# A fourth of the tokens take their value rows by index: the last matrix phase of a DiT block with 16,384 single-neuron experts

## The chip, the cores and the metric

The kernel runs on one core of one Trainium2 chip, as one program. The metric is the time of one execution on the device in microseconds (us); of several runs the median counts. The engines of the core are named as in the profile: PE is TensorE (matrix products; PEld its weight loads), DVE is VectorE, ACT is ScalarE, POOL is GpSimd, and SP issues most transfers.

## The reference

One transformer block is computed for 256 latent tokens of width 2048 (with 256 context tokens beside them in the attention part). What matters here is its last part, an expert layer in which each expert is one pair of rows, u and v. For each token, 8 heads choose 16 of 16,384 experts each, so 128 experts per token:

```
def peer(h, w_q, sub_keys, u, v):
    ...
    top_s, pos = lax.top_k(cand, PEER_TOPK)
    idx = jnp.take_along_axis(cidx, pos, axis=-1)
    g = jax.nn.softmax(top_s, axis=-1)
    ...
        act = jax.nn.gelu(jnp.einsum('cd,ced->ce', hc, u_sel))
        wts = (gc * act.astype(jnp.float32)).astype(v.dtype)
        return jnp.einsum('ce,ced->cd', wts, v[ic])
```

The expert index is a pair (i1, i2), each from 0 to 127: i1 names a tile of 128 experts, i2 the row in it. After this part come the gated residual (the gate g2 is one of six vectors that a product with w_ada gives, the "ada" vectors) and a final RMS norm.

## The kernel before, in words

The kernel does not look rows up. It computes all 16,384 experts for all 256 tokens, and zeroes what was not chosen. The weights of all phases lie one after another in one array, `stream`, in units of 128x1024 f32 (512 KB), and SP loads them in that order into a ring of four buffers (`raw`). Each unit is two halves of 128x512. For each half, ACT writes the rounded high part (`w_hi`, L367), DVE the rest (`w_lo`, L1008), and PE multiplies; there are four slots for split halves, so ACT and DVE work at most four halves ahead of PE. A product is made of three matmuls in fp32r (L668): high x high, high x low and low x high. The counters `w_high`, `w_low` and `w_free` order this by halves.

**U phase** (`first_product`, 128 tiles). Each tile of 128 experts takes four halves of 12 matmuls of 128x256 (256 tokens are the moving columns). ACT applies GELU. Before tile 2 x ROUTE_AT the result goes into `A` ([128 experts, 128 tiles, 256 tokens]); from then on `route` also runs: for each group of four tokens, four f32 matmuls of one-hot tables (L925) give a 128x128 table of gates, and DVE multiplies it into `A` (L1450). With 64 groups, one for each of the 64 tiles from tile 64 on, the gates of all 256 tokens are in `A` when the phase ends.

**V phase** (from `open_banks(experts_in)` on, 128 tiles). Each tile again takes four halves. Now the experts' values are the stationary operand and the weights the 512 moving columns: for each half and each of two blocks of 128 tokens, three matmuls of 128x512 into the eight PSUM banks, which stay open over all tiles. The values of each tile are split into `p_hi` (ACT, L614) and `p_lo` (DVE, L1481). DVE's loop body is `value_turn`: two tiles, so eight halves of `w_lo` and two of `p_lo`. In 32 of these turns it also adds one piece of w_ada into a sum (`acc_v`, L1505); the pieces come in through SP's queue between the units.

**Tail.** The banks are copied to `y_tok`, 16 small f32 products with a vector of ones turn the ada sum into columns (`ada_columns`, L675), 32 transposes (L986) bring the result back to the feature-major layout, DVE adds the residual (L1540), and the norm and four stores follow. POOL does little: it zeroes sums, and makes the distances for the one-hot tables (L349).

## Time and profile before

| what | value |
|---|---|
| median of 3 runs | 2293.31 us (2292.7 to 2295.07) |
| the profiled execution's own time | 2292.91 us |
| its span, first to last instruction | 2291.1 us |
| PE busy | 2211.5 us, 97% of the span |
| DVE busy | 1587.5 us, 69% |
| ACT busy | 1211.5 us, 53% |
| POOL busy | 100.2 us, 4% |
| mean granted TensorE clock | 0.987 |
| moved by DMA | 453.26 MB, mean 198 GB/s |

Busy time is the sum of an engine's instruction durations with overlaps counted once, so that an engine whose instructions overlap can be busy all the time and still have room. For what one instruction costs in a row of its like, read the distance between starts. The chain of work that ended last tells which engine sets the time of each stretch; the windows tell how much room the others have.

### The profile page before, as it was taken

How to read it: one execution, taken by the hardware profiler on the slowest of the kernel's cores; microseconds unless marked ns; L12 is line 12 of the kernel's file. 1: busy time of each engine (PE TensorE's matmuls, PEld its weight loads, DVE VectorE, ACT ScalarE, POOL GpSimd, SP SyncE). 2: the span in 40 equal slices, each digit the busy share in tenths (PEclk: the TensorE clock that was granted, in tenths of full speed). 3: DMA queues.
4: the chain of work that ended last, by engine and by line, in shares of the span. 5: the costliest groups of instructions: out<-in, count | busy, mean ns of one | idle time of the engine just before them, and what ended most of it. 6: DMA issues, size and time to landing. Idle time of an engine off the chain costs nothing.

```text
span 2291.1 us, 43555 instructions
## 1 busy us (share of the span) xinstructions
PE 2211.5 (97%) x14034; PEld 1952.9 (85%) x14034; DVE 1587.5 (69%) x2903; ACT 1211.5 (53%) x2131; POOL 100.2 (4%) x87
## 2 busy tenths in 40 slices
PE   4899999899999999999999999999999999999997
PEld 0478887668989999999999999998888888888886
DVE  5377767786674688788578788785666666555554
ACT  3232234575454677777665565655555555555553
POOL 0000000000000000000211111110000000000000
PEclk8899999899999999999999999999999999999998
DMA  9878876202755455555544444445766766555652
GB/s 387 338 268 282 281 251 235 99 1 76 275 200 183 150 176 187 183 182 183 169 157 162 156 156 162 157 157 210 248 238 238 242 243 238 193 193 193 193 193 81
DMA packets 123891, 453.26 MB, mean 198 GB/s; under 512 B 14400, under 2 KB 15168, under 8 KB 123200
## 3 DMA queue, kind: packets, MB, share of 16 engines
q1 hardware_dynamic: 123840, 452.63, 58.1%
q8 instruction: 26, 0.43, 0.1%
q14 instruction: 25, 0.20, 0.0%
HBM read 448.38 MB, written 4.19 MB: 198 GB/s over the span
## 4 chain that ended last, share of the span: by engine, by line
PE 92%; DVE 4%; DMA 2%; issue 1%; ACT 0%; SPq 0%; DVEq 0%
PE PS L668 84%; PE PS L925 3%; DMA ada_t<-w_ada 1%; PE PS L824 1%; DVE st L1209 1%; PE PS L798 1%; PE PS L675 1%; PE PS L711 1%; PE PS L651 1%; DMA raw<-stream 1%; PE PS L812 1%; PE PS L912 0%; DVE ot L1544 0%; DVE oT_l L1322 0%; DVE O L1254 0%
## 5 line engine op out<-in xcount | busy, mean ns | idle before, releaser
L367 ACT ACTIVATE w_hi<-raw 128x512 fp32r<-128x512 f32 x1296 | 816.7, 631 | 901.8 <-PE PS L668 891.0
L1008 DVE TENSOR_TENSOR w_lo<-raw,w_hi 128x512 fp32r<-128x512 f32 x1296 | 884.5, 691 | 557.8 <-ACT w_hi L367 542.1
L668 PE MATMUL PS<-h_h,w_hi 128*128 128x256 f32 (+1 forms) x2304 | 657.8, 285 | 2.1 <-DVE h_l L1038 2.1
L668 PE MATMUL PS<-h_h,w_lo 128*128 128x256 f32 (+1 forms) x2304 | 651.8, 283 | 0.0
L668 PE MATMUL PS<-h_l,w_hi 128*128 128x256 f32 (+1 forms) x2304 | 651.7, 283 | 0.0
L668 PEld LDWEIGHTS PS<-h_h,w_hi 128*128 128x128 f32 x2304 | 441.9, 192 | 3.1 <-issue 2.6
L668 PEld LDWEIGHTS PS<-h_l,w_hi 128*128 128x128 f32 x2304 | 442.1, 192 | 0.0
L668 PEld LDWEIGHTS PS<-h_h,w_lo 128*128 128x128 f32 x2304 | 441.8, 192 | 0.0
L668 PE MATMUL PS<-w_hi,p_hi 128*128 128x512 f32 x1024 | 398.5, 389 | 0.0
L668 PE MATMUL PS<-w_hi,p_lo 128*128 128x512 f32 x1024 | 398.3, 389 | 0.0
L668 PE MATMUL PS<-w_lo,p_hi 128*128 128x512 f32 x1024 | 398.3, 389 | 0.0
L668 PEld LDWEIGHTS PS<-w_hi,p_hi 128*128 128x128 f32 x1024 | 192.2, 188 | 40.3 <-DVE p_lo L1481 0.4
L668 PEld LDWEIGHTS PS<-w_lo,p_hi 128*128 128x128 f32 x1024 | 192.2, 188 | 39.9
L668 PEld LDWEIGHTS PS<-w_hi,p_lo 128*128 128x128 f32 x1024 | 192.2, 188 | 39.9
L668 PE MATMUL PS<-w_hi,hl_h 128*128 128x512 f32 x288 | 113.9, 396 | 3.3 <-DVE w_lo L1008 3.3
L668 PE MATMUL PS<-w_lo,hl_h 128*128 128x512 f32 x288 | 113.3, 393 | 0.0
L668 PE MATMUL PS<-w_hi,hl_l 128*128 128x512 f32 x288 | 113.0, 392 | 0.0
L1023 DVE SCALAR_TENSOR_TENSOR acc<-ada,silu_c,acc 128x1024 f32<-128x1024 f32 x80 | 102.5, 1281 | 3.4
L349 POOL TENSOR_TENSOR hotB<-iota,i2T 128x512 f32<-128x512 f32 x64 | 78.0, 1219 | 371.4 <-PE PS L925 339.2
L1450 DVE TENSOR_TENSOR A<-A,PS 128x512 f32 (+1 forms) x64 | 87.9, 1374 | 0.0
L668 PE MATMUL PS<-w_hi,hc_h 128*128 128x512 f32 x160 | 65.5, 409 | 12.4 <-DVE w_lo L1008 12.4
L668 PE MATMUL PS<-oT_h,w_hi 128*128 x256 | 72.5, 283 | 0.0
(198 smaller groups left out, 2250.6 us busy)
## 6 DMA issues: line engine op xcount, KB each, us to landing
raw<-stream SPq DMA_DIRECT2D x648, 512.0 KB, 3.4
ada<-w_ada SPq DMA_DIRECT2D x96, 512.0 KB, 4.5
ada_t<-w_ada SPq DMA_DIRECT2D x64, 512.0 KB, 9.4
ada_v<-w_ada SPq DMA_DIRECT2D x32, 512.0 KB, 4.3
x_c<-x_ctx SPq DMA_DIRECT2D x1, 2048.0 KB, 7.7
x<-x_lat SPq DMA_DIRECT2D x1, 2048.0 KB, 15.1
x_scratch<-x SPq DMA_DIRECT2D x1, 2048.0 KB, 7.3
x<-x_scratch SPq DMA_DIRECT2D x1, 2048.0 KB, 8.6
```

The costliest lines, as they stand in the source:

```text
L349: nc.gpsimd.tensor_tensor(hotB[:], iota[:].unsqueeze(1).broadcast_to([P, 4, P]), i2T[:, bass.ds(t0, 4)].unsqueeze(2).broadcast_to([P, 4, P ...
L367: nc.scalar.activation(w_hi[:, (2 * j + hf) % SPLIT, :], raw[:, j, hf * HALF:(hf + 1) * HALF], ACT.Copy).then_inc(S["w_high"], 1)
L651: ins = mm(PS[:, NORM_BANK[r], 0:T], ones_sq[:], s[:, k, :], start=(k == 0), stop=(k == KT - 1))
L668: ins = mm(out_, l_, r_, start=(start and q == 0), stop=(stop and q == 2), skip_group_check=check)
L675: ins = mm(PS[:, bank, at_ + k:at_ + k + 1], total[:, c % 2, k * P:(k + 1) * P], ones[:], start=True, stop=True)
L711: ins = mm(PS[32 * j:32 * j + 2, ADA1_BANK[g % 2], :], silu_c[:, kt + j // 2, :], ada1_t[(n + j // 2) % ADA1][:, j % 2 * HALF:(j % 2 + 1) ...
L798: ins = mm(PS[:, 2 * qt + sub, :], q, kT[sub * DH:(sub + 1) * DH, k, :], start=True, stop=True)
L812: ins = nc.tensor.transpose(PS[:, 4 + s % 2, k * P:(k + 1) * P], pr[:, m % 2, slot, k * P:(k + 1) * P], ident[:])
L925: ins = mm(PS[:, 4 + s, q * P:(q + 1) * P], hotB[:, q, :], hotA[:, q, :], start=True, stop=True)
L1008: V_.tensor_tensor(w_lo[:, h % SPLIT, :], raw[:, h // 2 % RAW, at_:at_ + HALF], w_hi[:, h % SPLIT, :].bitcast(F32), ALU.subtract).then_inc ...
L1023: ins = V_.scalar_tensor_tensor(acc[:, c % 2, :], ada[:, kt % ADA, :], silu_c[:, kt, 0:1], acc[:, c % 2, :], ALU.mult, ALU.add)
L1450: V_.tensor_tensor(av, av, PS[:, 4 + s, :].rearrange("p (t i) -> p t i", t=4), ALU.mult).then_inc(S["routed"], 1)
```

## The change

The 256 tokens are parted: DENSE = 192 and PICKED = 64.

- V phase, tokens 0 to 127: as before, three matmuls of 128x512 for each half.
- V phase, tokens 128 to 191: their low and high parts stand side by side in one stationary tile of 128 columns (`p_hl`), so that two matmuls, with `w_hi` and with `w_lo`, do for them. The two parts of each token end in different PSUM partitions and are added in the tail, by a product with `fold` (two identities of 64, one over the other).
- V phase, tokens 192 to 255: no matmul. POOL fetches their chosen rows of v by index, from `stream` in DRAM. One step j fetches one chosen row for each of 64 tokens x 2 halves of their list, so 128 rows of 8 KB, in two indirect DMAs of 128x1024, and DVE adds weight x row into `mixed` (two instructions of 128x1024, L1592). There are 64 steps and four row buffers. The weights need the GELU values of these tokens: ACT stores that part of `A` to DRAM (`values`; two stores, of 128x80x64 and 128x48x64 f32, the second at the end of the U phase), and POOL fetches it back with 64 indirect DMAs of 128 single numbers (`picked`), in four groups of 16.
- Routing covers 48 groups of four tokens instead of 64, and begins at tile 80 instead of 64 (ROUTE_AT 40 instead of 32).
- The last 32 pieces of w_ada, added by DVE during the V phase before, are now added in the U phase, over eight of PE's double tiles from LATE_ADA_AT = 30 on, and the 16 small `ada_columns` products stand there too, not in the tail.
- About eleven small DVE instructions in the U phase make the indices. The residual comes back at another place of SP's queue.

The core of the diff:

```diff
@@ sync @@
+            for r in range(8):
+                units(34 + LATE_ADA_AT + r)
+                for q in range(ADA):
+                    ...
+                    sp.dma_start(ada_u[:, q, :], w_ada_flat[64 + n]).then_inc(ada_in[q], 16)
...
@@ gpsimd @@
+            def fetch_rows(j):
+                for hf, index in enumerate((row_near.bitcast(U32), row_far)):
+                    nc.gpsimd.indirect_dma_start(
+                        row_t[:, j % ROWS, hf * UNIT:(hf + 1) * UNIT], None, rows,
+                        bass.IndirectOffsetOnAxis(ap=index[:, j:j + 1], axis=0)).then_inc(row_in[j % ROWS], 16)
+            def fetch_value(j):
+                nc.gpsimd.indirect_dma_start(
+                    picked[:, j:j + 1], None, singles,
+                    bass.IndirectOffsetOnAxis(ap=value_at.bitcast(U32)[:, j:j + 1], axis=0)
+                    ).then_inc(pick_in[j // PICK_GROUP], 16)
+            pool.wait_ge(S["picks_in"], 48)
+            pool.wait_ge(S["far_ready"], 1)
+            pool.wait_ge(S["w_free"], 2 * U_V + SPLIT)
+            for j in range(ROWS):
+                fetch_rows(j)
+            pool.wait_ge(S["values_kept"], 32)
+            for j in range(PICK_GROUP):
+                fetch_value(j)
+            for j in range(ROWS, PICKED):
+                pool.wait_ge(S["mixed"], 2 * (j - ROWS) + 4)
+                fetch_rows(j)
+                for k in range(PICK_GROUP + 2 * (j - ROWS), min(PICK_GROUP + 2 * (j - ROWS) + 2, PICKED)):
+                    fetch_value(k)
@@ scalar @@
+            nc.scalar.dma_start(values[:, 0:2 * ROUTE_AT, :], A[:, 0:2 * ROUTE_AT, DENSE:T]).then_inc(S["values_kept"], 16)
...
+            act.wait_ge(S["gelu_in"], NE_TILES - 2 * ROUTE_AT + 2)
+            nc.scalar.dma_start(values[:, 2 * ROUTE_AT:NE_TILES, :], A[:, 2 * ROUTE_AT:NE_TILES, DENSE:T]
+                                ).then_inc(S["values_kept"], 16)
@@ tensor @@
-                    for t in range(QT):
-                        tok = slice(t * P, (t + 1) * P)
-                        ins = three(PS[:, 4 * t + h % 4, :], p_hi[:, i, tok], p_lo[:, i, tok], slice(0, HALF),
-                                    h % SPLIT, False, False, check=True)
+                    three(PS[:, h % 4, :], p_hl[:, i, 0:P], p_hl[:, i, DENSE:DENSE + P], slice(0, HALF), h % SPLIT,
+                          False, False, check=True)
+                    both = p_hl[:, i, DENSE + P:2 * DENSE + PICKED]
+                    for w in (w_hi, w_lo):
+                        ins = mm(PS[:, 4 + h % 4, :], both, w[:, h % SPLIT, :], start=False, stop=False,
+                                 skip_group_check=True)
...
-            ada_columns(6, 3, acc_v)
-            ada_columns(7, 3, acc_v, 8)
...
+                if c == 0:
+                    pe.wait_ge(S["mixed"], 2 * PICKED + 2)
...
-                    for t in range(QT):
-                        ins = nc.tensor.transpose(turned(k)[:, t * P:(t + 1) * P], y_tok[:, t, k * P:(k + 1) * P], ident[:])
+                    nc.tensor.transpose(turned(k)[:, 0:P], y_tok[:, 0, cols], ident[:])
+                    mm(turned(k)[:, P:DENSE], y_tok[:, 1, cols], fold[:], start=True, stop=True)
+                    ins = mm(turned(k)[:, DENSE:T], mixed[:, cols], fold[:], start=True, stop=True)
@@ vector @@
+            def mix(r, s, hf):
+                cols = slice(hf * UNIT, (hf + 1) * UNIT)
+                if hf == 0:
+                    dve.wait_ge(row_in[s], 32 * r + 32)
+                dve.wait_ge(S["mixed"], 8 * r + (2 * s + hf + 1))
+                V_.scalar_tensor_tensor(mixed[:, cols], row_t[:, s, cols], weight[:, bass.ds(4 * r + s, 1)],
+                                        mixed[:, cols], ALU.mult, ALU.add).then_inc(S["mixed"], 1)
...
+            for b in range(3):
+                value_turn(0, b)
+            dve.wait_ge(S["values_kept"], 32)
+            dve.wait_ge(S["p_high_too"], 8)
+            dve.wait_ge(S["p_low"], 8)
+            V_.memset(mixed[:], 0.0).then_inc(S["mixed"], 2)
+            for g in range(PICK_GROUPS):
+                js = slice(g * PICK_GROUP, (g + 1) * PICK_GROUP)
+                dve.wait_ge(pick_in[g], 16 * PICK_GROUP)
+                link(V_.tensor_tensor(weight[:, js], picked[:, js], gate_at[:, js], ALU.mult))
+                bodies = PICK_GROUP // 4 - (g == PICK_GROUPS - 1)
+                with dve.Fori(0, bodies) as r:
+                    for s in range(4):
+                        value_turn(4 * r, 3 + g * PICK_GROUP + s, r + g * (PICK_GROUP // 4), s)
             split_low(161, 2)
             split_low(161, 3)
+            for s in range(4):
+                for hf in range(2):
+                    mix(PICKED // 4 - 1, s, hf)
```

PE, the first two halves of the V phase. Before, each half is two rounds of three matmuls, one for each block of 128 tokens:

```order
L668 MATMUL PS<-w_hi,p_hi 128x512
L668 MATMUL PS<-w_lo,p_hi 128x512
L668 MATMUL PS<-w_hi,p_lo 128x512
L668 MATMUL PS<-w_hi,p_hi 128x512
L668 MATMUL PS<-w_lo,p_hi 128x512
L668 MATMUL PS<-w_hi,p_lo 128x512
L966 REGISTER_ALU
```

PE, the same place after the change (L720 is the old L668; `p_hl` holds both parts of all 192 tokens):

```order
L720 MATMUL PS<-w_hi,p_hl 128x512
L720 MATMUL PS<-w_lo,p_hl 128x512
L720 MATMUL PS<-w_hi,p_hl 128x512
L1033 MATMUL PS<-w_hi,p_hl 128x512
L1033 MATMUL PS<-w_lo,p_hl 128x512
L1023 REGISTER_ALU
```

Five matmuls of the same shape stand where six stood, in each of 512 halves.

DVE, the start of the V phase after the change, with the counters that each instruction waits for (L1070 is the old L1008, L1583 the old L1481; three turns of 4 + 1 + 4 + 1 instructions stand ahead of the memset):

```order
L1070 TENSOR_TENSOR w_lo<-raw,w_hi 128x512 [waits w_high] x4
L1583 TENSOR_TENSOR p_hl<-A,p_hl 128x192 [waits p_high]
L1621 MEMSET mixed 128x2048 [waits p_high_too,p_low,values_kept]
L1625 TENSOR_TENSOR weight<-picked,gT 128x16 [waits pick_in0]
L1627 UNCONDITIONAL_BRANCH [waits dve]
L1627 ISA
L1070 TENSOR_TENSOR w_lo<-raw,w_hi 128x512 [waits w_high]
...
L1591 ISA [waits row_in0]
L1592 ISA [waits mixed]
L1592 SCALAR_TENSOR_TENSOR mixed<-row_t,weight,mixed 128x1024
```

After three turns DVE now waits for the stored values (`values_kept`) and for the first 16 fetched columns of them (`pick_in0`), with all later `w_lo` queued behind; then each turn has two instructions on `mixed`, the first of which waits for its row.

POOL, from the last one-hot distance on, after the change (before, one memset of `acc_v` stood here):

```order
L368 TENSOR_TENSOR hotB<-iota,i2T 128x512
L373 REGISTER_ALU
L373 COMPARE_AND_BRANCH
L383 DMA row_t<-stream,i1T 128x1024
L383 DMA row_t<-stream,row_far 128x1024
...
L388 DMA picked<-values_scratch,i2T 128x1 x16
L383 DMA row_t<-stream,i1T 128x1024
L383 DMA row_t<-stream,row_far 128x1024
L388 DMA picked<-values_scratch,i2T 128x1 x2
```

POOL issues 8 row fetches, then 16 value fetches, then 56 times two row fetches; the first 24 of these have two value fetches behind them.

## Rows read from the trace of the kernel before

**Rows 1.** The page, part 4: the chain that ended last, by engine and line.
```profile
PE 92%; DVE 4%; DMA 2%; issue 1%; ACT 0%; SPq 0%; DVEq 0%
PE PS L668 84%; PE PS L925 3%; DMA ada_t<-w_ada 1%; PE PS L824 1%; DVE st L1209 1%; PE PS L798 1%; PE PS L675 1%; PE PS L711 1%; PE PS L651 1%; DMA raw<-stream 1%; PE PS L812 1%; PE PS L912 0%; DVE ot L1544 0%; DVE oT_l L1322 0%; DVE O L1254 0%
```
**Rows 2.** The same chain in order of time: start us, us, what.
```profile
1208.97 0.89 PE PS L925 x8
1209.86 5.75 PE PS L668 x48
...
1559.35 1.90 PE PS L860 x8
1561.25 696.56 PE PS L668 x3072
2257.81 1.76 PE PS L864 x8
2260.24 5.17 PE PS L675 x32
```
**Rows 3.** Windows: stretch, us, busy (instructions) by engine, granted clock, DMA share, GB/s.
```profile
1000.00:1100.00 100.00, 100.00 (x834) 99.79 (x833) 77.96 (x144) 71.14 (x105) 13.23 (x8) 1.00 0.58 185
...
1700.00:1800.00 100.00, 100.00 (x442) 82.79 (x442) 66.77 (x102) 52.18 (x92) 0.00 (x0) 1.00 0.70 242
...
2100.00:2200.00 100.00, 100.00 (x443) 82.81 (x442) 57.09 (x93) 52.61 (x93) 0.00 (x0) 1.00 0.60 194
```
**Rows 4.** DVE's timeline in the V phase: start us, us, instruction, idle before.
```profile
1699.14 1.28 DVE L1505 SCALAR_TENSOR_TENSOR acc_v<-ada_v,modc,acc_v 128x1024 f32<-128x1024 f32 x1
1700.34 1.29 DVE L1008 TENSOR_TENSOR w_lo<-raw,w_hi 128x512 fp32r<-128x512 f32 x2
...
1709.08 0.69 DVE L1008 TENSOR_TENSOR w_lo<-raw,w_hi 128x512 fp32r<-128x512 f32 x1 [0.67 <-ACT w_hi L367]
1709.69 0.42 DVE L1481 TENSOR_TENSOR p_lo<-A,p_hi 128x256 fp32r<-128x256 f32 x1
1710.02 1.28 DVE L1505 SCALAR_TENSOR_TENSOR acc_v<-ada_v,modc,acc_v 128x1024 f32<-128x1024 f32 x1
```
**Rows 5.** The timeline of the tail.
```profile
2253.08 0.69 DVE L1008 TENSOR_TENSOR w_lo<-raw,w_hi 128x512 fp32r<-128x512 f32 x1 [0.61 <-ACT w_hi L367]
...
2259.59 0.69 DVE L1528 COPY y_tok<-PS 128x512 f32<-128x512 f32 x1 [5.82 <-PE PS L864]
...
2265.27 4.77 PE L986 MATMUL PS<-ident,y_tok 128*128 128x128 f32 x24
...
2266.48 1.66 DVE L1540 SCALAR_TENSOR_TENSOR x<-PS,mod,x 128x256 f32<-128x256 f32 x4 [0.19 <-PE PS L986]
...
2270.82 3.22 DVE L1540 SCALAR_TENSOR_TENSOR x<-PS,mod,x 128x256 f32<-128x256 f32 x8
```
**Rows 6.** Windows of the first 120 us, where the DMA engines are full.
```profile
30.00:40.00 10.00, 5.38 (x32) 0.41 (x24) 6.63 (x3) 0.00 (x0) 0.00 (x0) 0.67 1.04 406
...
80.00:90.00 10.00, 10.00 (x41) 6.06 (x41) 5.79 (x14) 3.24 (x7) 0.00 (x0) 0.77 1.01 406
...
110.00:120.00 10.00, 10.00 (x56) 5.04 (x55) 2.65 (x6) 0.60 (x1) 1.45 (x2) 0.91 1.03 413
```
**Rows 7.** DMA issues: size of each, median us from issue to landing.
```profile
raw<-stream SPq DMA_DIRECT2D x648, 512.0 KB, 3.4
...
outT<-ot SPq DMA_DIRECT2D x4, 512.0 KB, 2.6
...
silu_c<-par SPq DMA_DIRECT2D x1, 16.0 KB, 1.7
```
**Rows 8.** SP's issue of a unit, 1600 to 1700 us: ns, least, median and most.
```profile
L254 SPq DMA_DIRECT2D raw<-stream x37: 332/333/333, 1601.1 to 1699.1; - x37
```
**Rows 9.** The line of POOL's distances (L349): ns, least, median and most.
```profile
L349 POOL TENSOR_TENSOR hotB<-iota,i2T x64: 1041/1220/1327, 1133.1 to 1549.0; 128x512 f32<-128x512 f32 x64
```
**Rows 10.** DVE's timeline in the U phase, beside a distance of POOL.
```profile
1255.38 1.51 DVE L1008 TENSOR_TENSOR w_lo<-raw,w_hi 128x512 fp32r<-128x512 f32 x2 [1.04 <-ACT w_hi L367]
```

More of the change, by code:

```diff
@@ L353, in _ @@
             distance(0)
[L354 removed]
+            with pool.Fori(1, DENSE // 4) as g:
                 pool.wait_ge(S["route_used"], g)
                 distance(4 * g)
[L358 to L360 removed]
+            rows = stream.rearrange("u p n -> (u p) n")
+            singles = values.rearrange("p i t -> (p i t)").unsqueeze(1)
+            def fetch_rows(j):
[21 more added lines that the diff above has]
+                    fetch_value(k)
         @block.scalar
@@ L1425, in _, with both_parts @@
             dve.sem_inc(S["gates_ready"], 1)
-            next_low(2 * (U_U + 2 + 4 * (GATES_AT + 1)) - half[0])
-            low_turns(34 + GATES_AT + 1, ROUTE_AT - GATES_AT - 1)
+            up = slice(PICKED, P)
+            first, second, gate = sel[up, 1, 0, :], sel[up, 1, 1, :], sel[up, 1, 2, :]
+            def both_parts(a, dst, write):
+                write(near[up, a, :], 0)
+                link(write(dst[up], PICKED))
+            link(V_.tensor_tensor(spare[up], ident[up], iota[up], ALU.mult))
@@ new lines, in _ @@
+            link(V_.reduce_sum(place[up], spare[up], AX))
+            link(V_.tensor_scalar(place[up], place[up], -float(PICKED), None, ALU.add))
+            link(V_.scalar_tensor_tensor(spare[up], first, 2.0 * P, second, ALU.mult, ALU.add))
+            both_parts(0, row_near, lambda dst, c: V_.tensor_scalar(
+                dst.bitcast(U32), spare[up, c:c + PICKED], float(U_V * P), None, ALU.add))
+            link(V_.scalar_tensor_tensor(spare[up], second, float(NE_TILES), first, ALU.mult, ALU.add))
@@ new lines, in _ @@
+            dve.wait_ge(S["ada_zeroed"], 8)
+            for c in (6, 7):
+                b0 = 34 + LATE_ADA_AT + 4 * (c - 6)
+                with dve.Fori(0, 4) as r:
+                    for q in range(4):
+                        late_add(c, 4 * r, q)
+                        split_low(r + (b0 + q // 2), (q + 2) % 4)
+                dve.wait_ge(S["ada2_used"], 16 * c + 16)
+                dve.sem_inc(S["ada_sum"], 1)
+            low_turns(42 + LATE_ADA_AT, ROUTE_AT - LATE_ADA_AT - 8)
+            ada_keep(6, 6)
```

157 lines of the change are left out of this document (89 added, 68 removed).

## The prediction

> **What bounds the kernel now.** I read the chain of waits first: TensorE holds 92% of it, and the line of the three-part matmuls alone 84% [rows 1]. In order of time the V phase is one piece of 696.56 us with 3072 matmuls, and nothing in it is waited for [rows 2]; that is 0.2267 us for a matmul of 512 columns. The windows say how much room the others have there: TensorE 100 of 100 us at clock 1.00, VectorE 57 (67 while it adds w_ada pieces), ScalarE 53, and the DMA engines a share of 0.60 at 194 GB/s (0.70 at 242) [rows 3]. So fewer matmuls in V shorten the run by their own time, as long as nothing that is added takes the lead.
>
> **What is removed.** (1) Each of 512 halves loses one matmul of six, of unchanged shape: 512 x 0.2267 = **-116.1 us**. (2) 16 of 64 routing groups: a tile with a group has 0.89 us between its matmuls, 5.75 us for 48 of them [rows 2]; 16 x 0.89 = **-14.2 us**. VectorE's part of these groups lay under TensorE and counts nothing.
>
> **What is moved.** (3) The 16 column products of the ada sums take 5.17 us at the end [rows 2] and the same in the U phase, where TensorE sets the time: **+5.2 us** there. In the tail they are gone, but something takes their place: after the last `w_lo`, VectorE has 8 additions of rows to do. One of that shape takes 1.20 us from start to start (1699.14 to 1700.34) [rows 4], so 9.6 us. The banks are ready 2259.59 - 2253.77 = 5.8 us after the end of a late `w_lo` [rows 5], some 5 us with five matmuls for a half. VectorE so copies its first rows 4.6 us later and the transposes start 5.5 us after the banks close, where before it was 2265.27 - 2259.59 = 5.7 us [rows 5]: nothing gained or lost. (4) Transposes become one transpose and two f32 products with `fold`. An f32 product of 128 columns is two passes of 0.89/8 = 0.11 us [rows 2]; I take that for 64 columns too. Five passes for each of 16 k give 9 us, where VectorE's 0.40 us for one k (3.22/8) and its row copies [rows 5] set 7.6 us: **+2 us**. Without the moves and waits below, the profiled 2292.9 us become 2292.9 - 116.1 - 14.2 + 5.2 + 2 = **2169.8 us**.
>
> **w_ada in the U phase.** For each 24 matmuls of 256 columns (5.75/48 x 24 = 2.88 us [rows 2]) VectorE has one addition, 1.20 us, and two `w_lo`, 0.61 us each from start to start (1709.08 to 1709.69 [rows 4]): 2.4 us, hidden by TensorE. The transfers are 1.05 MB in 2.88 us, 364 GB/s for 92 us, where 185 GB/s flowed in U [rows 3]. The full DMA engines gave 406 to 413 GB/s [rows 6]. It fits, but with two kinds of load behind each other in SP's queue I add **+2 us** (0 to 10). The eleven index instructions cost nothing: VectorE has 22 of 100 us free there [rows 3] and four split halves lie ahead of TensorE.
>
> **VectorE in V.** A turn of two tiles is 40 x 0.2267 = 9.07 us for TensorE. VectorE has 8 `w_lo` (8 x 0.61), two `p_low` (0.33 us for 256 columns, 1709.69 to 1710.02 [rows 4], so 0.27 for 192) and two additions of 1.20: 7.8 us. It is full to 86%, not the bound. If it had no cover, its 60 pairs of additions would cost 144 us.
>
> **Transfers in V.** A turn needs 4 units and one row step, 6 x 0.524 MB, in 9.07 us: **347 GB/s**, against 406 to 413 [rows 6]. A 4 KB piece so costs an engine 16 x 4096 B / 406 GB/s = 0.161 us. A store of 512 KB lands in 2.6 us, a load of 128 pieces of 128 B in 1.7 us [rows 7]; with 8 pieces on each engine, 2.6 - 8 x 0.161 leaves 1.3 us of fixed time, and a small piece some 0.05 us. For the first 24 steps the two value fetches then take 16 x 0.05 = 0.8 us of the 9.07, beside 7.7 us of large pieces: 94%. I take **+5 us** of single delays.
>
> **The start of V, the dearest part.** VectorE's wait for values and the first 16 columns stands behind three turns. With the four halves split ahead, TensorE has 28 halves: 28 x 5 x 0.2267 = **31.7 us** of cover. What must happen in it:
> - the second store: 128 x 48 pieces of 256 B, 384 on each engine. At 0.05 us that is 19 us; by bytes alone 1.57 MB / 406 GB/s = 4 us; if each costs as much as a 4 KB piece, 62 us. Beside it the first four row steps take 64 x 0.161 = 10.3 us of each engine, and the stream 57% of them (231 of 406 GB/s) for 31.7 us, which leaves 13.6 us. Of 29.5 us of work 15.9 are left when TensorE runs dry, so the store lands at 47 us (9 if the pieces go by bytes, about 90 if they are dear).
> - 16 value fetches by POOL, one after another. No row shows an indirect DMA. From below, SP's issue is 0.33 us [rows 8]; from above, POOL's longest instruction of 128 partitions, 1.33 us [rows 9], behind one whole addition of VectorE, 1.28 us [rows 4]: 2.6 us. I take **1.3 us**, near POOL's own 1.22 us, since two engines that want the same memory hold each other up little: two `w_lo` took 1.51 us beside a distance [rows 10] and 1.29 without [rows 4]. So 20.8 us, and 1.7 us to land [rows 7].
> - one product for the weights and the next `w_lo`, 1.1 us.
>
> 47 + 20.8 + 1.7 + 1.1 = 70.6 us, less 31.7: TensorE stands still for **39 us** once (0 at the low ends, 103 at the high ones). After a gap of that kind the clock is not full at once: around 80 us, with TensorE idle before, 10 busy us ran at 0.77, between its two levels of 1.2 and 2.4 GHz [rows 6]. That is 2.3 us; I take **+3 us**. The later groups are fetched eight steps ahead and wait for nothing. POOL then has four fetches, 5.2 us, for a turn of 9.07.
>
> **Sum.** 2169.8 + 39 + 3 + 5 + 2 = **2218.8 us** against the profiled 2292.9. The median of the runs is 0.4 us above the profile, which is noise; I say **2219 us**, 3.2% less. A measurement tells a change of 0.2% (4.6 us) from none.
>
> **The rivals.**
> - *Little stall at the start* (0.17). Small pieces go by bytes and a fetch takes under 1 us: weights are there at 9 + 16 + 2.8 = 28 us, inside the cover. Then 2169.8 + 10 = **2180 us**. For it: the small load above landed in 1.7 us [rows 7]. Against: it is 16 KB, the store has 48 times the pieces.
> - *Transfers bound V* (0.19). Gathered rows go slower than the stream, or the two queues get in each other's way. At 330 GB/s, between the 347 needed and less, a turn is 9.53 us, 60 turns give +28 us: **2247 us**. For it: V asked for 194 and 242 GB/s before [rows 3], so that nothing there shows 347 beside the products. Against: 406 GB/s in pieces of the same 4 KB [rows 6].
> - *The stores hold SP's units up* (0.07). If the first store (640 pieces on each engine, 32 us at 0.05) keeps the stream's transfers back, TensorE stops in U as well, after the four buffers: +25 us, **2244 us**. Nothing before shows two issuing queues at once.
> - *POOL sets the pace and the kernel gets slower* (0.07). If a fetch waits for the gaps between VectorE's instructions, which read the same memory nearly without pause (7.8 of 9.07 us), POOL gets two in a turn, 4.5 us for one. V would last 47 + 176 x 4.5 + 12 = 851 us and the run 2169.8 + 851 - 580.5 = **2440 us**. It decides from a fetch of (703.6 - 59)/176 = 3.7 us on, with 703.6 us the length of V that takes the whole gain (2560 x 0.2267 = 580.5, and 2292.9 - 2169.8 = 123.1). Against: both engines kept their times nearly [rows 9, 10].
>
> On the last one a page speaks: the Trainium skill, "SBUF — State Buffer", section "A bandwidth-pool intuition that's wrong (but worth ruling out)", says that a transfer whose descriptors GpSimd writes takes about 3100 ns instead of 620 ns beside a VectorE copy that holds the shared port, because GpSimd is locked out until it ends. With 3.1 us for a fetch the first weights would come 68 us late and V end by VectorE's pace again, about 2248 us by that page. The trace before has no such transfer, and its distances beside VectorE (1.22 us median [rows 9]) speak against a factor of five. The same page says that VectorE instructions with two SBUF inputs shut out only GpSimd reads, which is the milder case here.
>
> **Chances and range.** The forecast (one stall of 20 to 60 us, the rest at TensorE's pace) 0.50, its own range 2198 to 2243; the rivals 0.17, 0.19, 0.07 and 0.07. From 2172 (almost no stall, almost no delays) to 2265 us (a stall of 85 us, or transfers at 320 GB/s) 8 in 10 are held. Faster by over 0.2%: all cases but the last, and a bad end of the third: 0.92. Within 0.2%: 0.02. Slower: 0.06.
>
> **What the profile after would show.** V: five matmuls in 1.13 us outside of gaps; if it is more, the releaser tells VectorE (additions longer than 1.28 us, or `w_lo` starts over 0.61) from a late `raw`. One long idle stretch of TensorE 32 us into V that ends by VectorE's `weight`; its length tests the store and the fetches apart (when `values` lands, and the distance of two value fetches on POOL). U: routing tiles only 48, no idle of TensorE in the w_ada stretch or after the first store. Tail: 5 to 6 us from the closed banks to the first transpose. I am wrong if a fetch takes over 2 us beside VectorE, if the stream's landing time grows from 3.4 to over 7 us, or if TensorE waits in every turn.

## The result and the profile after

| what | before | after |
|---|---|---|
| median, same chip | 2293.34 us (4 runs) | 2226.93 us (2224.07 to 2228.38) |
| ratio, 95% interval | | 0.9705 (0.9686 to 0.9724) |
| profiled execution | 2292.91 us | 2224.07 us, span 2221.9 |

One more execution took 2976.62 us at a mean granted clock of 0.652 instead of 0.975; it is left out of the ratio. The predicted 2219 us is 8 us below the median, and the range holds it. The change makes the kernel 3.0% faster. The profiled executions differ by 68.8 us, and that is made up as follows.

The page after, parts 1 and 4: busy time of each engine, then the chain that ended last, by engine and by line (the long last line of that part is left out). They answer to [rows 1]:

```profile
PE 2108.7 (95%) x13442; PEld 1852.3 (83%) x13442; DVE 1672.5 (75%) x2954; ACT 1212.7 (55%) x2243; POOL 301.7 (14%) x264
...
PE 71%; DMA 16%; DVE 7%; issue 3%; ACT 2%; POOL 1%; SPq 0%; DVEq 0%; ACTq 0%
```

TensorE held 92% of the chain in [rows 1]; now it holds 71%, and transfers 16%. So V is no longer one piece of TensorE as in [rows 2]. Where it breaks, the windows show (stretch, us, busy with instructions by engine, granted clock, DMA share, GB/s), beside [rows 3]:

```profile
1553.00:1580.00 27.00, 26.49 (x112) 20.45 (x113) 14.48 (x25) 14.17 (x31) 7.58 (x8) 1.00 1.05 376
1580.00:1606.00 26.00, 6.77 (x31) 5.32 (x29) 6.33 (x11) 5.55 (x12) 15.11 (x16) 0.68 0.27 90
1606.00:1650.00 44.00, 43.90 (x184) 35.83 (x185) 37.18 (x57) 25.59 (x53) 20.99 (x16) 0.95 0.81 287
1700.00:1800.00 100.00, 98.28 (x428) 79.51 (x427) 85.66 (x130) 59.90 (x128) 53.02 (x44) 1.00 0.92 331
...
2184.00:2188.00 4.00, 1.23 (x7) 1.26 (x8) 3.27 (x4) 0.00 (x0) 0.00 (x0) 0.85 0.00 0
2188.00:2196.00 8.00, 8.00 (x44) 8.00 (x43) 4.54 (x10) 3.23 (x8) 0.00 (x0) 0.50 0.01 2
2196.00:2204.00 8.00, 8.00 (x38) 7.65 (x38) 3.66 (x9) 3.54 (x10) 0.00 (x0) 0.51 0.00 0
```

Read three things here. From 1580 to 1606 us TensorE does 6.8 us of work: a stall where the prediction had one, half as long. From 1700 on it seems nearly full, but the number of matmuls tells more than the busy time, since busy matmuls overlap: 428 in 100 us, where 442 or 443 stood in [rows 3]. In the tail the clock is at half, 1.2 GHz, for 16 us.

The chain in order of time, around the stall (start us, us, what):

```profile
1546.96 2.88 PE PS L720 x24
1551.59 31.54 DMA values_scratch<-A
1583.39 0.95 POOL picked L388
1584.64 0.95 POOL picked L388
...
1600.87 0.95 POOL picked L388
1602.12 2.37 DMA picked<-values_scratch,i2T
1604.94 0.70 DVE w_lo L1070
1605.87 1.62 PE PS L720 x3
```

The second store, 16 fetches 1.25 us apart, a landing and the next `w_lo` stand one behind the other, as the prediction had them. DVE's timeline shows who waits (start us, us, instruction, idle before and its releaser):

```profile
1604.52 0.18 DVE L1625 TENSOR_TENSOR weight<-picked,gT 128x16 f32<-128x16 f32 x1 [18.39 <-DMA picked<-values_scratch,i2T]
1604.94 2.50 DVE L1070 TENSOR_TENSOR w_lo<-raw,w_hi 128x512 fp32r<-128x512 f32 x4 [0.25 <-DVE weight L1625]
```

The same chain in steady state repeats every 9.3 us, where 9.07 were due:

```profile
1841.77 7.00 DMA raw<-stream
...
1851.01 7.02 DMA raw<-stream
...
1860.27 7.05 DMA raw<-stream
...
1869.56 7.53 DMA raw<-stream
```

One unit of the stream in each turn takes 7 us and ends last. POOL's timeline says what was issued just ahead of two of them, 1849.14 and 1850.39 before 1851.01, 1858.24 and 1859.47 before 1860.27:

```profile
1849.14 0.94 POOL L383 DMA_INDIRECT row_t<-stream,i1T  x1 [6.73 <-DVE mixed L1592]
1850.39 1.26 POOL L383 DMA_INDIRECT row_t<-stream,row_far  x1 [0.30 <-issue]
1858.24 0.93 POOL L383 DMA_INDIRECT row_t<-stream,i1T  x1 [6.59 <-DVE mixed L1592]
1859.47 1.44 POOL L383 DMA_INDIRECT row_t<-stream,row_far  x1 [0.30 <-issue]
```

TensorE's own waits in V (line waited for: us in total, times, longest) come to the stall of 19.2 us and 21 short ones:

```profile
PE PS L720 <- DVE w_lo L1070: 29.5, 22, 19.2
...
ACT w_hi L412 <- DMA raw<-stream: 99.4, 70, 4.4
```

The second row is ACT from 1620 to 2120 us: it waits 70 times for a unit. ACT's wait passes through `w_hi` to DVE's `w_lo`, so for the short waits the first row names DVE where the transfer is the cause.

### The profile page after: what moved, and what is told of

Its sections match the earlier page's. It is cut to its first block, busy times and chain, and to the rows that moved or that the text cites. A ratio compares the mean times of both kernels' runs of the same rounds, so it can differ in the third digit from the quotient of the medians.

```text
span 2221.9 us, 42631 instructions
## 1 busy us (share of the span) xinstructions
PE 2108.7 (95%) x13442; PEld 1852.3 (83%) x13442; DVE 1672.5 (75%) x2954; ACT 1212.7 (55%) x2243; POOL 301.7 (14%) x264
## 4 chain that ended last, share of the span: by engine, by line
PE 71%; DMA 16%; DVE 7%; issue 3%; ACT 2%; POOL 1%; SPq 0%; DVEq 0%; ACTq 0%
PE PS L720 60%; DMA raw<-stream 13%; PE PS L1033 3%; PE PS L977 2%; DVE w_lo L1070 2%; DMA ada_t<-w_ada 2%; DMA values_scratch<-A 1%; ACT w_hi L412 1%; PE PS L876 1%; DVE st L1271 1%; PE PS L850 1%; PE PS L763 1%; PE PS L727 1%; PE PS L703 1%; POOL picked L388 1%
## 5 line engine op out<-in xcount | busy, mean ns | idle before, releaser
L412 ACT ACTIVATE w_hi<-raw 128x512 fp32r<-128x512 f32 x1296 | 805.2, 630 | 822.3 <-PE PS L720 547.3
L1070 DVE TENSOR_TENSOR w_lo<-raw,w_hi 128x512 fp32r<-128x512 f32 x1296 | 865.8, 689 | 386.3 <-ACT w_hi L412 368.2
L720 PE MATMUL PS<-h_h,w_hi 128*128 128x256 f32 (+1 forms) x2304 | 657.6, 285 | 3.1 <-DVE h_l L1100 2.1
L720 PE MATMUL PS<-h_h,w_lo 128*128 128x256 f32 (+1 forms) x2304 | 652.9, 283 | 0.0
L720 PE MATMUL PS<-h_l,w_hi 128*128 128x256 f32 (+1 forms) x2304 | 652.8, 283 | 0.0
L720 PEld LDWEIGHTS PS<-h_h,w_hi 128*128 128x128 f32 x2304 | 442.8, 192 | 4.2 <-issue 2.6
L720 PEld LDWEIGHTS PS<-h_l,w_hi 128*128 128x128 f32 x2304 | 442.9, 192 | 0.0
L720 PEld LDWEIGHTS PS<-h_h,w_lo 128*128 128x128 f32 x2304 | 442.7, 192 | 0.0
L720 PE MATMUL PS<-w_hi,p_hl 128*128 128x512 f32 x1024 | 405.0, 396 | 31.1 <-DVE w_lo L1070 29.5
L720 PEld LDWEIGHTS PS<-w_hi,p_hl 128*128 128x128 f32 x1024 | 193.2, 189 | 88.9 <-issue 46.7
L720 PE MATMUL PS<-w_lo,p_hl 128*128 128x512 f32 x512 | 200.6, 392 | 0.0
L1033 PE MATMUL PS<-w_hi,p_hl 128*128 128x512 f32 x512 | 200.2, 391 | 0.0
L1033 PE MATMUL PS<-w_lo,p_hl 128*128 128x512 f32 x512 | 199.9, 390 | 0.0
L1592 DVE SCALAR_TENSOR_TENSOR mixed<-row_t,weight,mixed 128x1024 f32<-128x1024 f32 x128 | 163.1, 1279 | 0.0
L383 POOL DMA_INDIRECT row_t<-stream,i1T x64 | 76.3, 1193 | 352.1 <-DVE mixed L1592 340.1
L720 PE MATMUL PS<-w_hi,hl_h 128*128 128x512 f32 x288 | 114.0, 396 | 3.2 <-DVE w_lo L1070 3.2
L1033 PEld LDWEIGHTS PS<-w_hi,p_hl 128*128 128x128 f32 x512 | 96.7, 189 | 20.6
L1033 PEld LDWEIGHTS PS<-w_lo,p_hl 128*128 128x128 f32 x512 | 96.6, 189 | 20.5
L720 PE MATMUL PS<-w_lo,hl_h 128*128 128x512 f32 x288 | 113.2, 393 | 0.0
L720 PE MATMUL PS<-w_hi,hl_l 128*128 128x512 f32 x288 | 113.2, 393 | 0.0
L720 PEld LDWEIGHTS PS<-w_lo,p_hl 128*128 128x128 f32 x512 | 96.8, 189 | 18.1
```

What stands on the lines that cost most here:

```text
L383: nc.gpsimd.indirect_dma_start(row_t[:, j % ROWS, hf * UNIT:(hf + 1) * UNIT], None, rows, bass.IndirectOffsetOnAxis(ap=index[:, j:j + 1], ...
L412: nc.scalar.activation(w_hi[:, (2 * j + hf) % SPLIT, :], raw[:, j, hf * HALF:(hf + 1) * HALF], ACT.Copy).then_inc(S["w_high"], 1)
L720: ins = mm(out_, l_, r_, start=(start and q == 0), stop=(stop and q == 2), skip_group_check=check)
L1033: ins = mm(PS[:, 4 + h % 4, :], both, w[:, h % SPLIT, :], start=False, stop=False, skip_group_check=True)
L1070: V_.tensor_tensor(w_lo[:, h % SPLIT, :], raw[:, h // 2 % RAW, at_:at_ + HALF], w_hi[:, h % SPLIT, :].bitcast(F32), ALU.subtract).then_inc ...
L1592: V_.scalar_tensor_tensor(mixed[:, cols], row_t[:, s, cols], weight[:, bass.ds(4 * r + s, 1)], mixed[:, cols], ALU.mult, ALU.add).then_inc ...
```

## The experiments

The first four leave out a part of the computation; the others compute all of it. "V" is the time from its first matmul, read to some 0.3 us, to the closing one (626.9 us after, 696.5 before), "tail" from there to the end of the span (42.4 us, before 33.4), "records" the matmuls counted from 1700 to 1900 us (856 after; 884 is the full pace). The start of V moves by up to 8 us between profiles whose U phases hardly differ (1552.6 to 1560.3 us), so V, tail and records are the finer measure, and single times are good to some 5 us. `rows_only`, `plain_rows`, `half_rows`, `pair_fetch` and `x2_late` are one execution each. The kernel before had medians of 2293.3 to 2297.1 us beside the different sets of runs, so a difference in us between two sets can be off by 4; the ratios are free of that. How far records scatter shows `tail_order`, whose V phase is that of the changed kernel: 852 instead of 856, and 832 instead of 835 from 1900 to 2100 us.

**Nothing gathered** (`no_rows`): no stores, no fetches, no additions of rows; five matmuls for a half stay.

```diff
-            for j in range(ROWS):
-                fetch_rows(j)
-            ...
-                        value_turn(4 * r, 3 + g * PICK_GROUP + s, r + g * (PICK_GROUP // 4), s)
+                        value_turn(4 * r, 3 + g * PICK_GROUP + s)
```

> Leaves out the picked quarter altogether: no store of values, no value fetches, no row fetches, no additions into the sum (tokens 192 to 255 get nothing from the experts). What is left is the shorter matrix part, the moved w_ada pieces, the 16 groups fewer of routing and the new tail. My terms for these, with the U phase as measured (8.3 us shorter), are 2292.9 - 8.3 - 116.1 and a tail near that of before plus 2 to 4 us: 2171 us, V in 580.5 us without a gap. The rival that TensorE's five matmuls are slower than five sixths of six (the stationary tile with both parts) would show as V longer than 582 us without any wait.

Measured: 2170.06 us, ratio 0.9459 (0.9441 to 0.9477); V 582.1, records 884, tail 29.8. Its windows:

```profile
1700.00:1900.00 200.00, 200.00 (x884) 165.73 (x884) 134.51 (x223) 128.88 (x265) 0.00 (x0) 1.00 0.70 231
```

The median is 0.3 us from the frame of the sum, 2169.8 us. Part of that is luck: the profiled execution took 2168.0 us, with V beginning 2.1 us later and lasting 1.6 us longer than the terms have it, and a tail of 29.8 us where they have 35.4 (33.4 + 2). The tail is short because no additions stand ahead of it, and not 2 to 4 us longer than before, as this run's expectation says. What the gathering costs is 2226.9 - 2170.1 = 57 us.

**Rows without values** (`rows_only`): rows are fetched and added, with the gates as weights; no store and no value fetch.

```diff
...
-                dve.wait_ge(pick_in[g], 16 * PICK_GROUP)
-                link(V_.tensor_tensor(weight[:, js], picked[:, js], gate_at[:, js], ALU.mult))
+                link(V_.tensor_copy(weight[:, js], gate_at[:, js]))
```

> Leaves out the store of the values and the value fetches, and weighs the rows by their gates alone; rows are fetched and added as in the change. The start's gap of 19 us must go. If the small pieces (value fetches) caused the late units of the stream, V comes near 581 us, the run near 2180 us. If the row fetches did, alone, V stays near 581 + 22 = 603 us and the run near 2200 us (the tail stays 9 us longer than before).

Measured: 2203.08 us, V 604.5, records 861. The stall is gone, but V is still 22.4 us longer than without rows: the row fetches make the units late, without the value fetches.

**The same bytes without an index** (`plain_rows`): as the run before, but each fetch is a plain transfer of 128x1024, issued by POOL.

```diff
-                    nc.gpsimd.indirect_dma_start(
-                        row_t[:, j % ROWS, hf * UNIT:(hf + 1) * UNIT], None, rows, ...)
+                    nc.gpsimd.dma_start(row_t[:, j % ROWS, hf * UNIT:(hf + 1) * UNIT],
+                                        stream[U_V + 2 * j + hf]).then_inc(row_in[j % ROWS], 16)
```

> As rows_only, but each row step is two plain transfers of 512 KB from one place, issued from POOL too, in place of 128 rows by index (the rows are those of one tile, not the chosen ones). Same bytes, same times of issue. If fetching by index is what makes rows dear, V comes near 581 us and the run near 2180 us; if it is the bytes or their coming in bursts, it stays within 3 us of rows_only.

Measured: 2192.71 us, V 591.8, records 875. With an index V is 12.7 us longer for the same bytes, so neither of the two expectations came true: part is the index, part the bytes. A fetch occupies POOL for 0.53 us instead of 0.94, and a row lands in 6.1 us instead of 7.6 (medians, 1750 to 2100 us). The index does not cost the DMA engines more time for a piece. This is POOL's queue from 1850 to 2100 us, `rows_only` and below it `plain_rows` (packets, MB, share of 16 engines):

```profile
q0 software_dynamic: 7350, 26.77, 31.1%
q0 software_dynamic: 7635, 27.83, 32.6%
```

0.311 x 16 x 250 / 7350 is 0.169 us for a piece with an index, and the second line gives 0.171. What is left was not separated: POOL's longer instruction, the later landing, or the addresses, which are scattered in the one run and lie together in the other.

**Half the bytes, all the additions** (`half_rows`): one indirect fetch for a step, and DVE adds its 1024 columns twice.

```diff
-                for hf, index in enumerate((row_near.bitcast(U32), row_far)):
+                for hf, index in enumerate((row_near.bitcast(U32),)):
...
-                V_.scalar_tensor_tensor(mixed[:, cols], row_t[:, s, cols], weight[:, bass.ds(4 * r + s, 1)],
+                V_.scalar_tensor_tensor(mixed[:, cols], row_t[:, s, 0:UNIT], weight[:, bass.ds(4 * r + s, 1)],
```

> As rows_only, but only the first half of each row is fetched, and both additions read it: half of the added bytes, all of VectorE's work. If transfers make TensorE wait, V comes to 581 to 584 us and the run to 2180 us. If VectorE's additions do, V stays near 603 us.

Measured: 2188.11 us, V 589.4, records 879:

```profile
1700.00:1900.00 200.00, 199.68 (x879) 164.42 (x878) 177.52 (x266) 126.53 (x264) 26.32 (x22) 1.00 0.84 289
1900.00:2100.00 200.00, 195.92 (x854) 160.82 (x853) 172.44 (x258) 123.24 (x257) 25.88 (x21) 0.99 0.84 290
```

VectorE is as busy as ever (177.5 of 200 us) and TensorE nearly full: the additions are not what V waits for. The second window, 25 records less, has the reload of x2, 2 MB in SP's queue between the units.

**The two halves of a step apart** (`split_fetch`), each when its half of the row buffer is free:

```diff
-                pool.wait_ge(S["mixed"], 2 * (j - ROWS) + 4)
-                fetch_rows(j)
+                for hf in range(2):
+                    pool.wait_ge(S["mixed"], 2 * (j - ROWS) + 3 + hf)
+                    fetch_rows(j, (hf,))
```

> The changed kernel, but POOL issues the first half of row j as soon as the first addition has freed its half of the buffer, and the second half after the second addition, some 4.5 us later, with one value fetch behind each. Same bytes, half the burst. If the stream's units come late because a burst of 1 MB stands ahead of them, about half of the 22 us go: V after the first gap near the pace of 872 or more matmul records in 200 us (856 in the change, 884 at full pace), the run near 2213 us. If the loss is the rate that this mix of transfers reaches, nothing changes: 2225 us within 3.

Measured: 2218.48 us, ratio 0.9658 (0.9642 to 0.9674); V 620.6, records 858. The theory of the burst asked for 2213 us and 872 records or more; neither came. The time gains 8 us and V 6.3, but 858 records against 856 are within the scatter, so that no gain is shown from 1700 to 1900 us.

**Two steps at once** (`pair_fetch`), so 2 MB in every second turn:

```diff
-                pool.wait_ge(S["mixed"], 2 * (j - ROWS) + 4)
+                if j % 2 == 0:
+                    pool.wait_ge(S["mixed"], 2 * (j + 1 - ROWS) + 4)
```

> The changed kernel, but POOL issues two row steps (2 MB) together in every second turn. Same bytes, twice the burst. By the burst theory V loses another 10 to 20 us: 2235 to 2245 us. By the rate theory it stays at 2225 us within 4.

Measured: 2239.83 us, V 638.1, records 842 at 328 GB/s. The same bytes in a coarser rhythm cost 13 us more, as the theory of the burst has it: the time hangs on how the transfers lie, not on their sum alone.

**Early store** (`early_store`): the second store is cut in three; only the last two tiles' values are stored at the end of U.

```diff
+            for b0, b1 in ((ROUTE_AT, 60), (60, 63), (63, 64)):
+                with act.Fori(b0, b1) as b:
+                    ...
+                if b1 < 64:
+                    act.wait_ge(S["gelu_in"], 2 * b1 - 2 - 2 * ROUTE_AT + 2)
+                    nc.scalar.dma_start(values[:, kept[-1]:2 * b1 - 2, :], A[:, kept[-1]:2 * b1 - 2, DENSE:T]
+                                        ).then_inc(S["values_kept"], 16)
```

> The changed kernel, but the store of the last 48 tiles' values is cut into three, of 38, 6 and 4 tiles, issued while the U phase still runs; only the last, of 512 pieces of 256 B, is left at the start of V. Its 31.5 us should become 3 to 8, hidden behind POOL's eight row fetches (10 us); the 16 value fetches take 20 us as before, so the weights are there some 33 us into V, where TensorE runs dry at 34. The gap of 19.2 us and the two low-clock stretches beside it (3 us) go: 2203 us. If instead the gap is not the store's but the fetches' (descriptors or landing), it shrinks by less than 10 us.

Measured: 2213.24 us, ratio 0.9634 (0.9618 to 0.965); the longest wait of TensorE at the start of V (to 1700 us) is 3.0 us instead of 19.2. The value fetches begin at 1569.24, not 1583.39, and now lie beside VectorE's work: 24.1 us for the 16 with their landing, 21.1 before. Of 24 us expected 14 came. Part of the rest is behind the start: records fell to 849, and from 1700 us on TensorE waits 14.6 us, up to 5.6 at a time, where the changed kernel waits 9.0. Why the steady part got worse is not shown.

**x2 late** (`x2_late`): the reload stands behind the last unit in SP's queue.

```diff
+            with sp.Fori(X2_AT, U_END // 4) as b:
+                units(b)
             sp.wait_ge(S["p_low"], 80)
             sp.dma_start(x2[:], x2_dram).then_inc(S["x2_in"], 16)
-            with sp.Fori(X2_AT, U_END // 4) as b:
-                units(b)
```

> The changed kernel, but the residual (2 MB) is loaded back after the last unit of the stream instead of 14 blocks before. In the changed kernel units landed in 11 us at that place and TensorE waited. If the transfers are at their limit in V, those bytes cost their own time, 2.1 MB at 340 GB/s, so 4 to 6 us: 2219 us. If only chance put the two together, no change. It must land before the residual is added, some 20 us later; if it does not, the tail gets longer.

Measured: 2219.87 us; records from 1900 to 2100 us 852 instead of 835, which is 3.9 us, and V 6.8 us shorter.

**Another order of the tail** (`tail_order`): ACT copies all eight banks, PE turns and folds them while VectorE still adds its last rows, and the folds of `mixed` follow.

```diff
+                for t in range(QT):
+                    nc.scalar.activation(y_tok[:, t, c * HALF:(c + 1) * HALF], PS[:, 4 * t + c, :], ACT.Copy
+                                         ).then_inc(S["y_kept_a"], 1)
...
+            pe.wait_ge(S["mixed"], 2 * PICKED + 2)
+            for k in range(KT):
+                ins = mm(turned(k)[:, DENSE:T], mixed[:, k * P:(k + 1) * P], fold[:], start=True, stop=True)
```

> Only the tail is changed: ScalarE copies all eight banks of sums, TensorE turns and folds them while VectorE still adds its last eight rows, and the 16 folds of the gathered sums follow behind. Theory (the tail's 42.4 us are a wait of 5 us for the last additions, during which TensorE's clock falls, and 16 k at 0.96 us instead of 0.57): the wait is filled with work, the clock stays near full, the tail is 33 to 36 us, V is unchanged at 627 us and the run is 2219 us (2216 to 2222), ratio to before 0.967. Rival (the tail is set by ScalarE's and VectorE's copies and by the chain of sums behind them, and the clock is low whatever stands there): ScalarE's eight copies take as long as the additions did, the tail stays at 41 to 44 us and the run at 2226 us.

Measured: 2216.74 us, ratio 0.967 (0.965 to 0.969); V 626.3 (unchanged), tail 30.2 instead of 42.4. Its windows, against the last two of after:

```profile
2182.00:2186.00 4.00, 2.82 (x19) 1.62 (x19) 4.00 (x4) 2.13 (x5) 0.00 (x0) 1.00 0.02 7
2186.00:2194.00 8.00, 8.00 (x76) 7.92 (x76) 6.57 (x13) 4.99 (x12) 0.00 (x0) 1.00 0.01 2
```

76 matmuls in 8 us at clock 1.00, where after has 44 at 0.50; TensorE's wait ahead of the first transpose is 1.2 us instead of 5.3. The 12 us are the wait and the half clock behind it; ACT's copies do not set the tail.

**The three together** (`all_three`): early store, x2 late, other tail.

> The early store, the late reload of x2 and the other order of the tail together. Theory (the start of V, the bytes of the reload in V and the tail are three costs at three places that do not cover each other): the gains of 14, 7 and 8 us add up, 2226.9 - 29 = 2198 us (2193 to 2203), ratio to before 0.958. Rival (late units are one pool of lost time: what is won at one place comes back as waiting at another, as the early store gave 14 where 24 were due): 2208 us or more, ratio 0.963.

Measured: 2191.73 us, ratio 0.9553 (0.9536 to 0.9571), 35 us under after, where the three alone give 13.7 + 7.1 + 10.2 = 31. They add up within what the medians can tell (2198 us was foretold, 2193 at the least), and the rival of 2208 us is out.

**And the halves apart** (`all_split`).

> As the run before it, and the two halves of a row step are fetched apart, each when its own half of the tile is free. Theory (a burst of 1 MB in POOL's queue holds the next unit of the stream back): as alone, another 8 us less, 2190 us (2186 to 2195), ratio 0.955. Rival (the mean rate of the mixed transfers is the limit, not the bursts, and splitting only helped at the uneven start of V that the early store has already mended): 2197 us, the same as the run before within 3 us.

Measured: 2178.64 us, ratio 0.9495 (0.9478 to 0.9512); V 598.9 instead of 605.2, records 858 instead of 849, and 867 instead of 849 from 1900 to 2100 us. 13 us less, more than the 8 expected; but in the profiles only 6.3 of 13.5 us lie in V, and the other 7.2 are its earlier start (1553.1 against 1560.3 us), which comes before the first row fetch. So some 6 us are shown for the split.

**Eight units under way** (`deep_stream`): in the last 44 of V's 64 turns every second block of four units goes to a second set of buffers.

```diff
+        more = at("more", [P, RAW, UNIT], F32, R + 8 * KB)
...
+            with sp.Fori(0, 22) as m:
+                for a, (dst, sems) in enumerate(((more, more_in), (raw, raw_in))):
+                    for j in range(RAW):
+                        sp.wait_ge(S["w_low"], 16 * m + (8 * (117 + a) + 2 * (j - 3)))
+                        sp.dma_start(dst[:, j, :], stream[8 * m + (4 * (118 + a) + j)]).then_inc(sems[j], 16)
```

> The run with the split row steps, and in the last 44 of V's 64 turns a second set of four unit buffers, in memory that the value tiles already used leave free: eight units of the stream are under way instead of four. Work, bytes and rates asked for are the same. Theory (the transfers keep up on the mean, and what is left of late units is their uneven landing against a buffer only four units deep): the second set covers them, the 17 us that V still has over the version without gathering shrink by 44/64 of it, to 5 or 6 us, and the run is 2168 us (2164 to 2172), ratio to before 0.945; matmul records in 1700 to 1900 us rise from 858 only after the 20th turn, and in 1900 to 2100 us reach 880 or more. Rival (at 336 GB/s with gathered rows among them the transfers are at their own mean rate, so that a deeper buffer is only emptied later): 2177 to 2180 us, ratio 0.9495, the records stay at 865.

Measured: 2174.82 us, ratio 0.9476 (0.9461 to 0.9491); V 585.8. Its windows, and below them those of `all_split` for the same stretches:

```profile
1700.00:1900.00 200.00, 200.00 (x884) 165.62 (x883) 179.09 (x267) 128.87 (x265) 86.54 (x70) 1.00 0.97 358
1900.00:2100.00 200.00, 200.00 (x884) 165.58 (x884) 178.68 (x266) 129.60 (x267) 61.70 (x44) 1.00 0.94 347
```

```profile
1700.00:1900.00 200.00, 197.28 (x858) 159.44 (x857) 172.46 (x261) 120.86 (x258) 85.35 (x68) 1.00 0.93 336
1900.00:2100.00 200.00, 198.48 (x867) 161.69 (x866) 175.25 (x262) 123.62 (x260) 58.45 (x44) 1.00 0.94 341
```

884 records in 200 us is the number of the version that gathers nothing. The waits of ACT from 1800 to 2100 us, first with eight units under way, then `all_split` with four:

```profile
ACT w_hi L421 <- PE PS L1074: 99.4, 199, 0.5
```

```profile
ACT w_hi L414 <- PE PS L1044: 59.4, 119, 2.4
ACT w_hi L414 <- DMA raw<-stream: 53.0, 54, 2.1
```

ACT no longer waits for a unit once, although the same bytes flow beside it and a unit takes no less time to land (median 6.7 us, 6.3 with four). So the transfers keep up on the mean, and what counted was how late a unit lands against a ring of four. Whether it is the longer landing (3.3 us without gathering, 6.3 with it) or its spread (4.4 to 9.4 us) is not separated, since eight buffers cover both. The time does not follow as far as expected: 2168 was foretold, and 3.8 us of gain in the medians, with intervals that overlap, is not certain. V is 13.1 us shorter in the profile. Of these, 2.9 lie in its first 183.6 us (787 matmuls against 774), before the second set is used, and are chance or early scatter; the other 10.2 lie in the stretch with eight buffers, where 44/64 of 17 us, so 12, were due. But V began 5.3 us later, and the profiled execution of `all_split` was its slowest (2184.0 against 2176.69 to 2180.23).

## Why the prediction was right, step by step

The sum came out right in its frame and in total, but two of its terms erred against each other, the stall by 20 us too long and the transfers by 20 us too short: V was foretold to be 69.1 us shorter (-116.1 + 39 + 3 + 5) and is 69.6 us shorter. That V fits to 0.5 us is luck; what was right is that fewer matmuls shorten the run by their own time, less one stall and some late units.

- **What is removed** (-116.1, -14.2) and **what is moved** in U (+5.2): shown by `no_rows`, V 582.1 us against 580.5 and the whole 2170.06 against 2169.8, with the luck told there. The moved products have a price that the sum lacks: behind them the clock is 0.60 from 1204 to 1208 us, with TensorE busy all the time.
- **w_ada in U** (+2): V's first matmul comes 8.3 us earlier than in [rows 2]; the terms of U give 7.0, and the scatter of V's start is too wide to tell the two apart. The stretch costs nothing that shows: from 770 to 1233 us TensorE waits 1.0 us in all, and 347 GB/s flowed from 1100 to 1200 us.
- **VectorE in V**: its additions take 1279 ns in the mean, as in [rows 4]. Not the bound, shown by `half_rows` and `deep_stream` (178.7 of 200 us busy and TensorE at 884 records).
- **The start of V** (39): 19.2 us. The fetches were right (1.25 us apart against 1.3; 19.7 us against 20.8), the cover nearly so (34.0 us against 31.7: TensorE ran dry at 1586.6). The step that failed is the second store: 47 us were taken, and it landed 30.5 us after V's start. The DMA view from 1540 to 1620 us (packets, MB, share of 16 engines; q10 is the store's queue) gives both sizes of the working:

```profile
q1 hardware_dynamic: 3037, 11.06, 38.1%
q0 software_dynamic: 1808, 4.73, 15.9%
q10 hardware_dynamic: 6160, 1.57, 8.9%
```

  A large piece took 0.381 x 16 x 80 / 3037 = 0.161 us, as worked out. A piece of 256 B took 0.089 x 16 x 80 / 6160 = 0.0185 us, not 0.05: 384 of them are 7.1 us of an engine, not 19. With that price the prediction's own bookkeeping gives 10.3 + 7.1 - 13.6 = 3.8 us of work left when TensorE runs dry, so a landing at 35.5 us instead of 47: the price of a piece is 12 of the 16.5 us by which the step was off. The rest is the sharing: while the store ran (1553 to 1583 us) the stream took 46% of the engines and not 57%, the rows 35%, the store 24% (105% together, by the profile). By bytes alone, 0.0101 us for a piece, the same bookkeeping gives 32 us and not the 9 that the prediction wrote, so that its first rival, with 28 us, did not follow: 32 + 16 + 2.8 = 51 us would have been a stall of 19 us even then.
- **The clock behind the stall** (+3): 0.95 in the mean over the 44 us from 1606 us on, 2.2 us. It is one short piece at half clock:

```profile
1606.00:1610.00 4.00, 4.00 (x10) 3.14 (x11) 3.59 (x6) 0.63 (x1) 0.00 (x0) 0.50 0.59 164
1610.00:1614.00 4.00, 4.00 (x19) 3.29 (x18) 2.06 (x4) 2.50 (x6) 0.00 (x0) 1.00 0.54 179
```

- **Transfers in V** (+5): this is the term that was too small. V's excess of 46.4 us over 580.5, less 19.2 and 2.2, leaves 25 us. The step that failed is "94% of a turn, so single delays": a unit that is issued behind POOL's 1 MB lands in 7 us, not 3.4, and with four buffers that is once in each turn a little too late. Shown by the experiments: 22.4 us stay when only rows are fetched (`rows_only`), 9.7 when they go without an index (`plain_rows`), 7 come back when x2 moves (`x2_late`), and none are left in steady state with eight buffers (`deep_stream`). That the burst of 1 MB is what makes the unit late is borne out by `pair_fetch` and `all_split`, but not by the records of `split_fetch`; so the late unit is shown, and the burst as its cause only in part. More than half of the 22.4 us goes with the index or the scattered addresses, for which the sum had no term.
- **The tail** (+2): +9.0 us. The transposes began 5.3 us after the banks closed, as foretold, but then each k took 0.96 us (first transposes at 2186.77, 2187.72, 2188.68) instead of the 0.56 of the working (9 us / 16). The step that failed is the price of a pass, taken at the full clock: the clock was at 0.50. It had also been 0.50 at the same place before, for a shorter while (2264 to 2268 us), there without a wait of that length: it was 1.00 from 2260 to 2262 us and 0.57 from 2262 to 2264, while TensorE, busy 2.00 of 2.00 us, ran the 32 one-column passes of the ada sums. In the changed kernel `tail_order` shows that the wait is to blame.
- **The rivals.** That of bound transfers (2247 us) was half right: 331 to 341 GB/s flowed in V, the number it named, and a turn took 40/4.28 = 9.35 us. But the rate was a result and not a limit: `deep_stream` moved 358. The stores held nothing up in U. POOL never set the pace: a row fetch took 1.14 us in the mean. (With four row buffers and 64 steps, two row fetches follow 60 times, not 56 as the section on the change says. So 184 fetches stand where this rival has 176: its V would be 47 + 184 x 4.5 + 12 = 887 us and the run 2476 us, and it would decide from a fetch of 3.5 us on.) The page "SBUF — State Buffer" of the Trainium skill, section "A bandwidth-pool intuition that's wrong (but worth ruling out)", has 3100 ns instead of 620 ns, a factor of five, for such a transfer beside a VectorE copy. Here a row fetch took 0.93 to 2.02 us beside a busy VectorE, and a value fetch 0.94 us beside an idle one, so that the direction shows and the size does not. The copy of that page was not run here: the instructions beside the fetches read two SBUF inputs. In `all_split` the median of a row fetch is 1.41 us and the longest 3.22.
- **The signs of being wrong** came close: one row fetch of 2.02 us; units that landed in 6.1 us in the median, and the late one of each turn in some 7 to 8 (1700 to 1900 us); and 70 waits of ACT for a unit in some 53 turns.

What stays open: how the index costs time, since its pieces take the engines no longer; and how much of the late unit is the burst. That V starts up to 8 us apart is older than any store or fetch of the V phase: in `all_three` the first routing matmul stands at 1241.1 us and in the changed kernel at 1233.4, and V starts 319 us behind it in both. The granted clock goes with it: 0.66 from 550 to 560 us, 0.83 from 660 to 670 and 0.71 from 1210 to 1220 in `all_three`, where the changed kernel has 1.00 in all three. Why the clock differs there is open. The best version, `deep_stream`, is 2.3% faster than the changed kernel (2174.82 against 2226.93 us) and 5.2% faster than the one before.

## What to carry to other kernels

Where added transfers bring the DMA engines to over 90%, don't ask only whether the mean rate suffices: look at how long the last unit of a ring takes behind the largest burst, and give the ring that depth. Cutting the burst helped less surely (6 us of V in both tries). Where a phase needs data from the very end of the one before, send ahead all that is ready, so that only the last bit lies on the path. And a wait of 5 us ahead of a chain of small matmuls costs twice, for itself and for the clock behind it; work of any kind that fills it saves both.

## What the runs showed of the hardware

- Small stores cost an engine little (0.0185 us for a piece of 256 B) but last long beside full queues: 6144 pieces landed in 31.5 us, the first store's 10240 in 19.0 us in U, where the engines were busy to 0.98 with 276 GB/s (1229 to 1249 us).
- Indirect fetches of 128 pieces on POOL start 1.25 us apart, for 4 B and 4 KB alike (0.94 us and 0.30 us of issue); a plain transfer took 0.53 us of POOL. A fetched piece of 4 KB took a DMA engine 0.17 us with and without an index.
- With index rows and the stream in separate queues 358 GB/s flowed for 200 us, against 406 to 413 from SP's queue alone [rows 6].
- TensorE, idle for 5.3 us ahead of a chain of small f32 products, ran 16 us of it at 0.50 (1.2 GHz); after the 19.2 us stall, with matmuls of 512 columns behind it, it ran 4 us at 0.50 and then at 1.00.
- The clock also falls without idle time: 32 one-column passes stand from 1200.0 to 1203.4 us, and TensorE, busy 4.00 of 4.00 us, has 0.60 from 1204 to 1208 and 1.00 behind it.
